# Forget gate of the second layer in four column groups of TensorE, its running sums per block, and the first turn of the second attention written out

## The reference, cut to what matters

```
h = rms_norm(x, g) * (1 + scale) + shift          # scale, shift: one per sequence (prompt, sample)
q, k, v, g, f = split(h @ w_in)                   # f: 16 columns of 4112, one per head
logf = log_sigmoid(f + b_forget)                  # also an output
cum  = cumsum(concat(past_logf, logf))            # over tokens; past only for the sample tokens
logit = q.k / 8 + cum_q - cum_key                 # causal, then softmax, times v
o = attention * sigmoid(g);   x = x + gate * (o @ w_out)
```

## Time and profile before

| | |
|---|---|
| median of 3 runs | 1533.2 us (1532.76 to 1535.65) |
| the profiled execution: its own time | 1533.63 us |
| its span, first to last instruction | 1531.5 us |
| TensorE (PE) busy | 1492.0 us, 97% |
| VectorE, ScalarE, GpSimd busy | 70%, 41%, 38% |
| chain that ended last, by engine | PE 86%, DVE 7%, ACT 3% |

### The profile page before, as it was taken

How to read it: one execution, slowest core, us unless ns; L and a number is a source line. 1 busy time by engine, 2 the same in 40 slices (tenths; PEclk the granted TensorE clock), 3 DMA queues, 4 the chain that set the end, 5 groups by cost and what they waited for, 6 DMA issues and landing times.

```text
span 1531.5 us, 29136 instructions
## 1 busy us (share of the span) xinstructions
PE 1492.0 (97%) x11405; PEld 1373.2 (90%) x11405; DVE 1069.4 (70%) x2057; ACT 634.3 (41%) x1265; POOL 580.4 (38%) x346
## 2 busy tenths in 40 slices
PE   5999999999999999999999999999999999999998
PEld 2768956899999999999888888887999999999998
DVE  1659888668887778876644444457988877688753
ACT  3434366344552145522533333334254541355423
POOL 1234841225771066722322222231227640376421
PEclk8999999999999999999999999999999999999999
DMA  9874510341344433452254444443532355333521
GB/s 335 269 264 150 141 39 2 96 114 40 104 128 159 148 83 89 116 173 67 77 167 127 127 127 127 127 128 100 171 91 56 93 168 167 86 108 83 156 79 62
DMA packets 244454, 189.21 MB, mean 124 GB/s; under 512 B 12888, under 2 KB 228608, under 8 KB 240112
## 3 DMA queue, kind: packets, MB, share of 16 engines
q1 hardware_dynamic: 231232, 178.61, 38.9%
q10 hardware_dynamic: 13104, 8.97, 1.9%
HBM read 175.44 MB, written 8.50 MB: 120 GB/s over the span
## 4 chain that ended last, share of the span: by engine, by line
PE 86%; DVE 7%; ACT 3%; issue 2%; DMA 1%; POOL 0%; ACTq 0%; SPq 0%; POOLq 0%; DVEq 0%
PE lin L860 40%; PE lin L1440 28%; PE lin L877 5%; PE S L1201 2%; PE O L995 1%; PE O L1331 1%; PE O L1254 1%; DVE acc_out L2666 1%; PE T L1234 1%; PE S L1064 1%; DMA ada_raw<-in_w_ada 1%; PE S L1120 1%; ACT act_hi L1665 1%; PE lin L1300 1%; PE T L1291 0%
## 5 line engine op out<-in xcount | busy, mean ns | idle before, releaser
L2147 POOL TENSOR_TENSOR w_lo<-w_raw,w_hi 128x1024 fp32r<-128x1024 f32 (+3 forms) x68 | 168.3, 2476 | 409.6 <-ACT w_hi L1612 409.6
L2238 POOL TENSOR_TENSOR w_lo<-ada_raw,w_hi 128x512 fp32r<-128x512 f32 x114 | 156.9, 1378 | 241.8 <-ACT w_hi L1913 241.8
L1612 ACT ACTIVATE w_hi<-w_raw 128x1024 fp32r<-128x1024 f32 (+2 forms) x110 | 125.2, 1139 | 224.7 <-PE lin L860 212.3
L860 PE MATMUL lin<-act_hi,w_hi 128*128 128x288 f32 (+1 forms) x1088 | 164.6, 302 | 5.3 <-ACT act_hi L1644 2.0
L860 PE MATMUL lin<-act_hi,w_lo 128*128 128x288 f32 (+1 forms) x1088 | 167.3, 299 | 0.2
L860 PEld LDWEIGHTS lin<-act_hi,w_hi 128*128 128x128 f32 (+1 forms) x1088 | 149.5, 189 | 15.5 <-issue 10.1
L860 PE MATMUL lin<-act_lo,w_hi 128*128 128x288 f32 (+1 forms) x1088 | 162.1, 298 | 0.0
L860 PEld LDWEIGHTS lin<-act_hi,w_lo 128*128 128x128 f32 (+1 forms) x1088 | 149.9, 188 | 7.5 <-issue 6.7
L860 PEld LDWEIGHTS lin<-act_lo,w_hi 128*128 128x128 f32 (+1 forms) x1088 | 149.6, 188 | 3.4 <-issue 2.9
L2238 POOL TENSOR_TENSOR w_lo<-s_tmp,w_hi 128x512 fp32r<-128x512 f32 x76 | 129.2, 1717 | 15.0 <-ACT w_hi L1916 15.0
L1440 PE MATMUL lin<-act_hi,w_hi 128*128 128x288 f32 x608 | 105.4, 295 | 0.0
(11 more groups left out here) (347 smaller groups left out, 3031.1 us busy)
## 6 DMA issues: line engine op xcount, KB each, us to landing
ada_raw<-in_w_ffn_in SPq DMA_DIRECT2D x76, 512.0 KB, 5.2
w_raw<-in_w_ffn_out SPq DMA_DIRECT2D x32, 704.0 KB, 4.9
ada_raw<-in_w_ada SPq DMA_DIRECT2D x20, 1024.0 KB, 7.6
ada_raw<-in_w_ada SPq DMA_DIRECT2D x32, 512.0 KB, 5.0
w_raw<-in_w_in_b SPq DMA_DIRECT2D x32, 512.0 KB, 4.2
w_raw<-in_w_in_a SPq DMA_DIRECT2D x16, 512.0 KB, 6.2
ada_qo<-in_w_ada SPq DMA_DIRECT2D x8, 1024.0 KB, 7.5
ada_raw<-in_w_ada_final SPq DMA_DIRECT2D x16, 512.0 KB, 5.6
```

Of the source, the lines that this page charges most:

```text
L860: last = nc.tensor.matmul(lin_u(u)[0:m, tok], w, (lo if p == 2 else hi)[:, at(t) if at else t, tok], start=(p == 0 and t == 0), stop=(p == ...
L1612: A(w_hi[:, u % 2, 0:n], w_raw[:, u % 2, 0:n], ACT.Copy).then_inc(whi_done, 1)
L2147: TT(w_lo[:, u % 2, 0:n], w_raw[:, u % 2, 0:n], w_hi[:, u % 2, 0:n].bitcast(F32), ALU.subtract)\
L2238: TT(ring(w_lo, q), raw, ring(w_hi, q).bitcast(F32), ALU.subtract).then_inc(ws_lo_p, 1)
```

## The change

The forget gate is no longer a unit of its own; `U_FG` is gone and every later unit number is one lower.

- SyncE loads the 16 forget columns, unrounded, into a zeroed piece `wf` (32 columns for each feature tile) of `ada_row`. GpSimd zeroes it, and `bias_f`, early.
- `first_units` now runs `U_B` and `U_B+1`, with a call in the second half: `forget_gate`, 16 full float32 matmuls of `wf` with `fo` in four column groups (feature tiles 0 to 3, then 4 to 7 added, for two halves of the tokens), and eight with the two shift columns.
- ScalarE makes a bias of the shift's product and `b_forget`, and adds it in three pieces. The four partial sums are added by five matmuls with `fold_w`, which also bring them to token-major.
- The running sums go block by block, 128 columns each, and VectorE adds the last column of the block before (`carry_on`): seven chained steps in place of two.
- The sums stand behind the first four steps of `U_B+3`, between the two `k_tokens`.
- On ScalarE `split_hi(U_B + 2)`, the copies of `U_B` and `U_B+1` stand ahead of the exponential and logarithm of the gate.
- TensorE's first turn of `b_body` is written out ahead of the loop, and in its first block parts 0 and 1 of the filling unit stand ahead of the first `t_unit`, part 2 alone behind the second.

```diff
@@ in first_units
+                if late is not None:
+                    late()
                 for p in (1, 2):
...
@@ SyncE
             wb = i["w_in_b"][0]
-            w_load(U_FG, wb[:, 4096:4112], KT, 16)
+            sp.wait_ge(wf_zero, 1)
+            sp.dma_start(wf[:, :, 0:16], wb[:, 4096:4112].rearrange("(t p) n -> p t n", p=P)).then_inc(wf_in, 16)
...
@@ TensorE
-            first_units(U_FG, 16, 2, ACT_N2)
-            pe.wait_ge(lin_free[U_FG % 2], free_count(U_FG))
+            def forget_gate():
+
+                pe.wait_ge(wf_in, 16)
+                pe.wait_ge(y_done, y_base(2, 1) + KT)
+                for r in range(2):
+                    for h in range(2):
+                        for j in range(4):
+                            kt = 4 * r + j
+                            nc.tensor.matmul(S[32 * j:32 * j + 32, h, 0:HALF], wf[:, kt, :],
+                                             fo[:, kt, h * HALF:(h + 1) * HALF], start=(r == 0), stop=(r == 1))
+                for r in range(2):
+                    for j in range(4):
+                        kt = 4 * r + j
+                        last = nc.tensor.matmul(S[32 * j:32 * j + 32, 0, HALF:HALF + 2], wf[:, kt, :],
+                                                mods[:, SHIFT[2] + kt, :], start=(r == 0), stop=(r == 1))
+                last.then_inc(fg_done, 1)
+
+            first_units(U_B, P, 2, ACT_N2, forget_gate)
+            pe.wait_ge(z_done, 1)
             t_use(T_LF)
+            zf = zb[:, :, :].rearrange("p a c -> p (a c)")
             for t in range(5):
                 c = t * P if t < 4 else TOK - P
-                last = nc.tensor.transpose(T[:, t * 16:(t + 1) * 16], zb[:, c:c + P], ident[0:16, 0:16])
+                last = nc.tensor.matmul(T[:, t * 16:(t + 1) * 16], zf[:, c:c + P], fold_w[:, 0:16], start=True, stop=True)
...
                 for b in range(4):
-                    last = nc.tensor.matmul(S[0:16, 0, b * P:NP_], lf_tok[:, b, :], sums_w[:, 0:NP_ - b * P],
-                                            start=(b == 0), stop=(b == 3))
+                    last = nc.tensor.matmul(S[0:16, 0, b * P:(b + 1) * P], lf_tok[:, b, :], sums_w[:, 0:P],
+                                            start=True, stop=True)
...
                 for b in range(2):
-                    nc.tensor.matmul(S[0:16, 1, b * P:PAST + NS], lfc[:, b, :], sums_w[:, 0:PAST + NS - b * P],
-                                     start=(b == 0), stop=False)
+                    nc.tensor.matmul(S[0:16, 1, b * P:(b + 1) * P], lfc[:, b, :], sums_w[:, 0:P], start=True, stop=True)
...
-            lin_part(U_B + 1, None, KT, P, act_hi, act_lo, some=LIN_STEPS[0:18])
-            running_sums()
-            lin_part(U_B + 1, None, KT, P, act_hi, act_lo, some=LIN_STEPS[18:])
             linear(U_B + 2)
...
             gate_steps(0, 4)
+            running_sums()
             k_tokens(1, 0, U_B + 1, T_B0)
...
+                        ahead = first and r == 0 and k == 0
+                        if ahead:
+                            lin_part(u, 0, KT, P, act_hi, act_lo)
+                            lin_part(u, 1, KT, P, act_hi, act_lo)
                         t_unit(k, 0, r, n, t, it, 8, 26, pr_b, ps_b)
...
-                            lin_part(u, 0, KT, P, act_hi, act_lo, it, 8)
+                            lin_part(u, 2 if ahead else 0, KT, P, act_hi, act_lo, it, 8)
...
-                        for half in range(2 if nxt else 0):
+                        for half in range(2 if nxt and not ahead else 0):
...
-            with pe.Fori(0, PAIRS // 2 - 1) as it:
+            b_body(0, False, True)
+            with pe.Fori(1, PAIRS // 2 - 1) as it:
@@ ScalarE
-            act.wait_ge(mm_done, U_FG + 1)
-            A(zb[:, :], lin_u(U_FG, NB)[0:16, :], ACT.Identity, bias=bias_f[:, 0:1])\
...
+            act.wait_ge(fg_done, 1)
+            A(bias_z[:, :], S[:, 0, HALF:HALF + 2], ACT.Identity, bias=bias_f[:, 0:1]).then_inc(bz_done, 1)
+            act.wait_ge(bz_done, 1)
+            A(zb[:, 0, :], S[:, 0, 0:HALF], ACT.Identity, bias=bias_z[:, 0:1])
...
@@ VectorE
-            chain(V.tensor_scalar(cum[:, 0:NP_], S[0:16, 0, 0:NP_], -1.0 / QSCALE, None, ALU.mult))
+            def carry_on(bank, c0, c1, at):
+
+                before = cum[:, at + c0 - 1:at + c0].broadcast_to([16, c1 - c0])
+                chain(V.scalar_tensor_tensor(cum[:, at + c0:at + c1], S[0:16, bank, c0:c1], -1.0 / QSCALE, before,
+                                             ALU.mult, ALU.add))
+
+            chain(V.tensor_scalar(cum[:, 0:P], S[0:16, 0, 0:P], -1.0 / QSCALE, None, ALU.mult))
+            for c in range(1, 4):
+                carry_on(0, c * P, (c + 1) * P, 0)
             dve.wait_ge(cum_done, 2)
-            chain(V.tensor_scalar(cum[:, NP_:], S[0:16, 1, 0:PAST + NS], -1.0 / QSCALE, None, ALU.mult))
+            chain(V.tensor_scalar(cum[:, NP_:NP_ + P], S[0:16, 1, 0:P], -1.0 / QSCALE, None, ALU.mult))
+            carry_on(1, P, 2 * P, NP_)
+            carry_on(1, PAST, PAST + NS, NP_)
```

More of the change, by code:

```diff
@@ L63 @@
 U_F0B = U_F0 + 2 * FULL + KT
-U_FG = U_F0B + KT
-U_B = U_FG + 1
+U_B = U_F0B + KT
 U_OB = U_B + 4 * PAIRS
@@ L283, in encoder_step @@
         mulA = sb("mulA", [P, 5, KT, 2])
-        bias_f = sb("bias_f", [16, 1])
+        bias_f = sb("bias_f", [P, 1])
+        bias_z = sb("bias_z", [P, 2])
         negmax = sb("negmax", [P, 4, 3])
@@ L1481, in running_sums @@
                 for b in range(2):
-                    nc.tensor.matmul(S[0:16, 1, b * P:PAST + NS], lfc[:, b, :], sums_w[:, 0:PAST + NS - b * P],
-                                     start=(b == 0), stop=False)
+                    nc.tensor.matmul(S[0:16, 1, b * P:(b + 1) * P], lfc[:, b, :], sums_w[:, 0:P], start=True, stop=True)
                 nc.tensor.matmul(S[0:16, 1, PAST:PAST + NS], lf_tok[P - NS:P, 4, :], sums_w[P - NS:P, P - NS:P],
-                                 start=False, stop=True).then_inc(cum_done, 1)
+                                 start=True, stop=True).then_inc(cum_done, 1)
             def k_tokens(half, par, kp, t, it=0, tper=0, per=0):
@@ L1546, in ob_early, with b_body @@
                     lin_part(U_OB, None, KT, P, act_hi, act_lo, ready=split_ready(ACT_OB), some=some)
-            def b_body(it, last_turn):
+            def b_body(it, last_turn, first=False):
                 for r in range(2):
@@ L2002, in _ @@
             out_stage(U_OA, N, N, 1)
-            ffn_stage(0, KT * 16, 2)
+            ffn_stage(0, N, 2)
             A(sink[:, 0:1], eps[0:16, 0:1], ACT.Exp)
-            act.wait_ge(mm_done, U_FG + 1)
-            A(zb[:, :], lin_u(U_FG, NB)[0:16, :], ACT.Identity, bias=bias_f[:, 0:1])\
-                .then_inc(lin_free[U_FG % 2], 1)
-            split_hi(U_B + 1, N)
-            act.wait_ge(t_free, T_LF + 1)
-            A(lf_e[:, :], lf_e[:, :], ACT.Exp).then_inc(lf_act, 1)
-            A(sink[:, 1:2], eps[0:16, 0:1], ACT.Ln)
-            act.wait_ge(lf_dve, 4)
-            A(lf_l[:, :], lf_u[:, :], ACT.Ln).then_inc(lf_act, 1)
             def q_evac(par, u, it=0, per=0, cut=HALF):
@@ L2058, in v_tokens_evac @@
                     .then_inc(kv_sent, 16)
-            q_evac(0, U_B, cut=NB)
-            A(sink[:, 2:3], eps[0:16, 0:1], ACT.Exp)
-            split_hi(U_B + 2, N)
-            act.wait_ge(mm_done, U_B + 2)
-            A(kS_b[:, 0, 0:NP_], lin_u(U_B + 1)[:, 0:NP_], ACT.Copy)
-            A(kS_b[:, 0, NP_ + PAST:NK], lin_u(U_B + 1)[:, NP_:TOK], ACT.Copy)\
-                .then_inc(lin_free[(U_B + 1) % 2], 1)
-            split_hi(U_B + 3, N)
+            act.wait_ge(fg_done, 1)
+            A(bias_z[:, :], S[:, 0, HALF:HALF + 2], ACT.Identity, bias=bias_f[:, 0:1]).then_inc(bz_done, 1)
+            act.wait_ge(bz_done, 1)
+            A(zb[:, 0, :], S[:, 0, 0:HALF], ACT.Identity, bias=bias_z[:, 0:1])
+            A(zb[:, 1, 0:HALF - NS], S[:, 1, 0:HALF - NS], ACT.Identity, bias=bias_z[:, 0:1])
+            A(zb[:, 1, HALF - NS:HALF], S[:, 1, HALF - NS:HALF], ACT.Identity, bias=bias_z[:, 1:2])\
+                .then_inc(z_done, 1)
+            split_hi(U_B + 2, N)
+            q_evac(0, U_B, cut=NB)
+            act.wait_ge(mm_done, U_B + 2)
+            A(kS_b[:, 0, 0:NP_], lin_u(U_B + 1, NB)[:, 0:NP_], ACT.Copy)
+            A(kS_b[:, 0, NP_ + PAST:NK], lin_u(U_B + 1, NB)[:, NP_:TOK], ACT.Copy)\
+                .then_inc(lin_free[(U_B + 1) % 2], 1)
+            act.wait_ge(t_free, T_LF + 1)
+            A(lf_e[:, :], lf_e[:, :], ACT.Exp).then_inc(lf_act, 1)
+            A(sink[:, 1:2], eps[0:16, 0:1], ACT.Ln)
+            act.wait_ge(lf_dve, 4)
+            A(lf_l[:, :], lf_u[:, :], ACT.Ln).then_inc(lf_act, 1)
+            split_hi(U_B + 3, N)
+            A(sink[:, 2:3], eps[0:16, 0:1], ACT.Exp)
             v_evac_b(U_B + 2)
@@ L2272, in _ @@
             pool.wait_ge(out_sent, 16 * 6)
+            nc.gpsimd.memset(wf, 0.0).then_inc(wf_zero, 1)
             out_stage(U_OA, N, 1)
-            ffn_stage(0, KT * 16, 2)
-            for c in range(5):
```

(2 more changed lines are left out.)

13 lines of the change are left out of this document (9 added, 4 removed).

## The result

The changed kernel takes 1536.48 us in the median (1534.99 to 1538.96); the kernel before, run beside it, 1533.15 us. The ratio is 1.0021, with a 95% interval of 1.0014 to 1.0028. The forecast was 1531.5 us with a range from 1528.2 to 1535.0.

The account below looks back on a forecast made before the run. TensorE, busy nearly throughout, was taken as the bound: 11.04 us out, 5.4 in, 0.44 wait covered, 6.1 gained without waits; late transfers left 1.7. Median 1533.2 less 1.7 gave 1531.5 us, range 1528.2 to 1535.0.

Parts of the forecast that it names:

- the products: TensorE, after the gate: five products with a whole 128-column stationary operand, to token-major, ten records, 1.3 us added.
- the sums: TensorE: running sums taken per block, 832 columns at 1.7 ns plus 0.25 for starts, 1.65 us.
- the seven steps of `cum`: VectorE: chained running-sum steps of 0.32 us each, 2.2 us together, from 762.2 to 764.4.
- the write: Running sums' write on SyncE's queue: between 1.8 and 3.3 us, taken as 2.5, so bias loads issue at 766.9.
- the bias's way to the first maximum: From the bias loads' issue, the second `bk` load lands about 5.0 us later; first maximum starts at 771.9.
- The rival of bare weight loads: In the gate, 32 weight loads of 0.108 us lie uncovered, costing 3.4 us; time 1534.9 us, chance 0.04.
- The larger wait: TensorE, block 1's second transposes: waits 3.3 us because `U_B+5`'s weights land at 783.3; transposes at 785.5.
- The wait at the first transposes: TensorE, block 0's first transposes: ready at 775.5, transposes at 776.6, a wait of about 1.1 us.
- the gate is done at 758.4: VectorE's gate chain takes 5.1 us as before; TensorE reaches the sums at 761.1, 2.7 us in hand, no wait.
- rival 2: TensorE's clock falls to half during the wait: 3.4 us lost, 1534.9, or 6.8 lost, 1538.3; chance 0.20.
- up to 744.70 nothing differs for TensorE: Ahead of the gate: units take each other's places with equal matmuls and columns; the longer weight split costed at nothing.
- I see nothing that gives more back or takes more: Beyond block 1's second transposes: each block has its own filling, so the gain stays 1.7 us.

Follow-up runs that it names:

- first experiment: The changed kernel with GpSimd's zeroing of `acc_mid` moved behind the split of `U_B+4`'s weights instead of `U_B+2`'s; 1534.53 us, ratio 1.0008 to the kernel before.

## Why the prediction was wrong, step by step

Right were the sizes of what is added: the gate 2.17 us for 2.45, the products 1.04 for 1.3, the sums 1.62 for 1.65; the seven steps of `cum` 2.08 for 2.2; the write 2.13 for 2.5; the bias's way to the first maximum, 5.0 for 5.0. The rival of bare weight loads (3.4 us more) is refuted by the gate's 2.17, with 32 loads of 106 to 110 ns inside it. The larger wait was forecast at 3.3 us for the weights of `U_B+5` and is 3.42 us, for them, at that place. The wait at the first transposes was forecast at 1.1 us and is not there, since TensorE came later itself.

**The step that failed first** is "the gate is done at 758.4 ... the sums start at 761.1, with 2.7 us in hand. No wait." I took the chain's 5.1 us from before, and moved the chain without asking what GpSimd does at its new place. Before, it met one split (1.70 us, already in the 5.1). In the changed kernel it meets the zeroing of `acc_mid` and another split, and takes 9.5 us: 4.3 longer, of which the 2.7 in hand covered most and a wait of 1.65 was left. It cost 2.0 us by the ratios (first experiment). In the profiled execution the bias loads went out at 770.46, which is 767.9 on the old clock, for 766.9 forecast, and the second transposes ran at 786.8 for 785.5: the gain of 1.7 was 0.4.

**The second** is the choice between forecast and rival 2. The forecast had a wait of 3.3 us and the rows said that the clock was at half behind one of 2.60; giving the low clock only 0.20 was against my own rows. The rival happened as described, at a lower price than its 3.4: about 1.4 us in the medians, 2.6 us in the profiled execution. Its 6.8 us stood in none of the rows that I had; that low stretches were as long is luck; two of the five were 3.4. Since wait and clock go together, the weights' place in the queue was worth 4.7 us.

**The third** is "up to 744.70 nothing differs for TensorE". The order of instructions does not, but the buffers do: `bias_z` moves the hidden activations by 32 bytes against the weights. It is worth 0.8 us when undone in the changed kernel, 1.7 to 2.0 us when done in the kernel before; the intervals overlap, and the matmul times in the traces say 2.4. Of the 2.55 us lost ahead of the section in the profiled pair, 1.2 lie in layer 0's output stages; 1.1 are a wait near 204 us that also appears in executions of the old gate (with the pads of 8 and 16 bytes, and with the turn and early weights) and is missing in others of the new one, so it belongs to the execution.

The sum with these: -1.7 forecast, +1.3 for the later chain at the second transposes, +1.4 clock, +0.8 to 2.0 distance gives 1.8 to 3.0 us slower, against 3.3 measured with 2.1 to 4.3 as its interval. Of its terms the clock's stands on two differences that are not clear of noise, so its size is an estimate. "I see nothing that gives more back or takes more" was wrong in that a third cost was outside the section I read.

## What to carry to other kernels

When a chain moves, lay the other engines' rows beside its new place: here a VectorE instruction that took 0.52 us in one kernel took 3.97 beside a long GpSimd instruction, and moving the GpSimd work that nobody waited for mended it. A load that stands behind a wait on a computed value is late by all that delays that value; if its buffer is free, issue it ahead of the wait, and look at the granted clock behind a wait of TensorE before pricing it: here a wait of 3.4 us cost 4.7. After an edit that allocates a buffer, compare matmul times in stages that the edit does not touch before explaining anything there.

## What the hardware showed that was not expected

- The distance between the buffers of a matmul's two operands changes its rate: on 288 float32 columns 133.0 ns at the old distance and at 256 bytes more, 134.3 at 32 and 288 bytes more, 134.1 at 64 (`hid_hi` by `w_hi`; the bytes as I infer them). At 32 bytes more the products on `T_hi` and `T_lo` go from 132.9 to 133.3 and those on the normed activations stay within 0.1. Which part of 256 bytes counts was not tried.
- VectorE stood still until a GpSimd instruction was done: 3.97 us through the end of a split and a zeroing of 128 by 4096 float32, 2.32 beside a split of 128 by 1024.
- The clock was at half for 3.4 or 6.8 us around waits of 3.1 to 5.3 us. It also fell where no wait of TensorE stands just ahead: at 1112 to 1124 us in 11 of the 20 profiled executions (among them the kernel before, whose window stands below) and near 338 us in 12. Just ahead of both places TensorE runs products of one column (`ssq`, `sq`), and it is busy nearly throughout. These falls come and go between executions, so two single traces can differ by 1.7 us for them alone. What decides where the clock falls, and for how long, stays open.

```profile
1118.40:1125.30 6.90, 6.90 (x34) 6.90 (x34) 5.14 (x15) 2.82 (x10) 2.37 (x1) 0.51 0.54 151
```
